# Six extra matmuls on TensorE ahead of the expert loop of a hybrid decoder step

## The reference

```python
expert = g_idx * EXPERTS_PER_GROUP + e_idx
combine = jnp.sum(jax.nn.one_hot(expert, N_EXPERTS, dtype=jnp.float32) * weight[..., None], axis=-2)
a = jnp.einsum('btd,edf->btef', h, w_gate)
u = jnp.einsum('btd,edf->btef', h, w_up)
z = jax.nn.silu(a) * u * combine[..., None].astype(a.dtype)
return jnp.einsum('btef,efd->btd', z, w_down).astype(h.dtype)
```

## Time and profile before

| | |
|---|---|
| median of the runs | 633.3 us (631.67 to 634.66) |
| profiled execution | 632.5 us |
| its span, first to last instruction | 630.8 us |
| mean granted TensorE clock | 0.893 |
| TensorE busy with matmuls | 474.5 us (75%) |
| VectorE, ScalarE, GpSimd busy | 222.8, 149.1, 109.6 us |
| DMA | 168.82 MB, mean 268 GB/s |

### The profile page before, as it was taken

One profiled execution on the slowest core, in us unless ns is written; L12 is line 12 of the kernel. 1 busy time (PEld: TensorE's weight loads), 2 busy tenths in 40 slices (PEclk: granted clock), 3 DMA queues, 4 the chain that ended last, 5 costly groups with the idle time before them and its releaser, 6 DMA issues.

```text
span 630.8 us, 8583 instructions
## 1 busy us (share of the span) xinstructions
PE 474.5 (75%) x2852; PEld 241.1 (38%) x2853; DVE 222.8 (35%) x544; ACT 149.1 (24%) x313; POOL 109.6 (17%) x171
## 2 busy tenths in 40 slices
PE   1869999999977999973006883758888889788290
PEld 0448777788533445432002331212333333233130
DVE  0341554142694288998500011001111111111188
ACT  1221444524755212230001111001111111111053
POOL 5030001000274450000610111011111111111000
PEclk9969999999999999986557897678999999899595
DMA  8994865410674923107961799999999999995432
GB/s 276 403 354 189 263 223 197 162 47 0 252 299 136 423 29 133 68 2 300 422 250 57 289 424 421 421 421 421 423 397 415 387 365 418 406 399 209 175 131 102
DMA packets 44414, 168.82 MB, mean 268 GB/s; under 512 B 11594, under 2 KB 20866, under 8 KB 29006
## 3 DMA queue, kind: packets, MB, share of 16 engines
q1 hardware_dynamic: 36682, 146.48, 59.2%
q0 software_dynamic: 7360, 21.88, 9.4%
q10 hardware_dynamic: 340, 0.09, 0.1%
HBM read 162.05 MB, written 15.71 MB: 282 GB/s over the span
## 4 chain that ended last, share of the span: by engine, by line
PE 55%; DMA 20%; DVE 11%; issue 7%; ACT 3%; SPq 2%; POOL 1%; POOLq 1%; DVEq 0%
PE B L1527 16%; PE B L1788 15%; DMA wB<-in_w_up 11%; PE B L1813 6%; PE B L1697 5%; DMA ada_m<-in_w_ada 4%; PE B L1464 2%; DMA ada<-in_w_ada 2%; PE B L1596 1%; PE B L1767 1%; PE B L1539 1%; PE B L1625 1%; PE B L1666 1%; POOL table L635 1%; PE B L1835 1%
## 5 line engine op out<-in xcount | busy, mean ns | idle before, releaser
L1788 PE MATMUL B<-wA,XT 128*32 128x512 f32 x480 | 117.8, 647 | 44.2 <-DMA wB<-in_w_up 24.9
L1788 PE MATMUL B<-wB,XT 128*32 128x512 f32 x480 | 117.8, 648 | 0.0
L1527 PE MATMUL B<-hT,win 128*128 128x256 f32 (+1 forms) x448 | 104.0, 392 | 2.0 <-DVE hT L999 2.0
L1527 PEld LDWEIGHTS B<-hT,win 128*128 128x128 f32 x448 | 86.1, 194 | 22.5 <-issue 9.4
L1788 PEld LDWEIGHTS B<-wA,XT 128*32 128x32 f32 x480 | 34.6, 118 | 124.1 <-issue 124.1
L1390 DVE TENSOR_TENSOR z<-silu_g,B 128x256 f32<-128x256 f32 x15 | 6.3, 421 | 157.6 <-ACT silu_g L886 157.6
L1813 PE MATMUL B<-wA,zT 128*32 128x512 f32 x240 | 54.9, 599 | 2.6 <-ACT zT L888 2.3
L1813 PE MATMUL B<-wB,zT 128*32 128x512 f32 x240 | 54.9, 600 | 0.0
L1767 PE MATMUL B<-ident,X 128*128 128x128 f32 x128 | 22.6, 305 | 35.2 <-DMA X<-h_dram,gidx 32.9
L1697 PE MATMUL B<-wout,yT 128*128 128x512 f32 x112 | 48.8, 593 | 0.0
L886 ACT ACTIVATE silu_g<-B 128x256 f32<-128x256 f32 x15 | 5.8, 384 | 150.8 <-PE B L1788 150.8
(11 more groups left out here) (377 smaller groups left out, 616.8 us busy)
## 6 DMA issues: line engine op xcount, KB each, us to landing
wB<-in_w_gate SPq DMA_DIRECT2D x24, 1024.0 KB, 12.8
wB<-in_w_up SPq DMA_DIRECT2D x24, 1024.0 KB, 17.7
wB<-in_w_down SPq DMA_DIRECT2D x24, 1024.0 KB
ada<-in_w_ada POOLq DMA_DIRECT2D x12, 1024.0 KB, 7.2
ada<-in_w_ada SPq DMA_DIRECT2D x8, 1024.0 KB, 11.8
wA<-in_w_gate SPq DMA_DIRECT2D x8, 1024.0 KB, 14.9
wA<-in_w_up SPq DMA_DIRECT2D x8, 1024.0 KB, 18.1
wA<-in_w_down SPq DMA_DIRECT2D x8, 1024.0 KB
```

Of the source, the lines that this page charges most:

```text
L1527: last = pe.matmul(B[(q % 2) * 2 + h][:, 0:cn], win[:, n % 3, k, col:col + P], hT[:, k, c0:c0 + cn], start=(k == 0), stop=(k == KD - 1))
L1788: last = pe.matmul(B[2][32 * g:32 * g + 32, :], XT[:, k, 32 * g:32 * g + 32], gu[:, :, k, :], start=(k == 0), stop=(k == KD - 1))
```

## The change

Between the last matmul of the ranks (L1762) and the function transpose_X, TensorE gets a wait and six matmuls. The wait is for idx_in, the semaphore that the read of the index table raises. The matmuls load the 128x128 identity and stream a [128, 512] block of wout, float32, for k = 0 to 5. Each writes the whole bank B[3] anew, nothing reads the result, and none raises a semaphore. All else is as before.

```diff
             last.then_inc(rank_ps, 1)
 
+            pe.wait_ge(idx_in, 16)
+            for k in range(6):
+                pe.matmul(B[3][:, :], ident[:, :], wout[:, k, 0:512], start=True, stop=True)
+
             def transpose_X(p, half):
```

## The result

The kernel with the six blocks took 629.4 us (median of eight runs, 628.12 to 630.51) against 633.5 us for the kernel before in the same runs (630.84 to 635.08): a ratio of 0.994, 95% interval 0.9919 to 0.9962. That is 4.1 us less.

A forecast was written before the change was run, and what follows sets the result against it. No single resource was taken to bound the kernel; until 339.2 the path was TensorE at half speed. Terms +1.7 - 0.9 - 0.74 = +0.06 us on 632.5 gave 632.6, or 633.4 against the median; range 630.2 to 635.5.

The forecast's parts named there:

- The chain and its bound: Whole kernel: no single resource bounds it; a shift in the first down projection's end counts in full.
- The added work: Ahead of the first transposes: six blocks are twelve matmuls taking 7.3 us, and transposes start 1.7 us late.
- the transposes' gain: First eight transposes, at the high clock: 0.90 us back, with bounds of 0 and 0.90.
- the blocks' delay: First transposes, held up by the blocks: 1.7 us late (1.25 to 2.4), counted on the path.
- The pause: Between transposes and first gate and up: stays 2.52 us, loses the clock; gate and up 8.80 us, 0.74 back.
- clock kept: Rival: clock outlasts the pause ahead of gate and up, which takes 7.11 us; 631.7, or 630.7 with shorter pause; chance 0.32.
- The rule on the pauses: TensorE's pauses: three of three over 2.3 us lost the clock, none under 2 us did.
- The transposes at the high clock: First eight transposes: 1.04 us at the high clock against 1.94, despite the skill's rule; 0.90 us back.
- The steps behind keep their pauses and their low stretches: Steps behind the first gate and up: pauses and low-clock stretches unchanged, no term in the sum.
- The slow side of the forecast: Slower than the range: clock never rises (638.0), or late rise plus a later pause's fall (1.69 us each); chance 0.11.

The follow-up runs named there:

- e3_hold: Kernel before, without the six blocks, plus two blocks in step 0 between gate and up and the next transposes: 632.5 us against 631.6, ratio 1.0000.
- e1_nine: Changed kernel with nine blocks in place of six ahead of the first transposes: 633.4 us, ratio 1.0003 to the kernel before.
- e2_keep: Changed kernel plus one block at the end of every step, behind the down projection: 629.5 us, ratio 0.9922 to the kernel before.

## Why the prediction was wrong, point by point

**The chain and its bound** were right. An earlier end of the first down projection reached the end in full: the stretch from there to step 5 differs by 0.1 us.

**The added work** was right in its size: twelve matmuls (7.24 to 8.09 us in five profiles, against 7.3 worked out), transposes some 2 us behind the landing of the rows. It was right, too, that a float32 block is two matmuls. (Ahead of the prediction the description of the loop gives 64 and 32 matmuls for a step; these are instructions of the trace, and the code has 32 and 16 calls.) What was wrong is its price. "They then end 1.7 - 0.9 = 0.8 us later than now" was added to the path. The start of gate and up isn't bound to the transposes' end but to the landing of the rows, some 4.5 us on, and the delay (1.6 to 2.5 us in five profiles, against 1.7) cost nothing. So the bound of nothing that stood for the transposes' gain was the true value, and by the same reason the true value for the blocks' delay. The sum had +1.7 - 0.9 = +0.8 us where the profiles have -0.16 (a to b).

**The pause** is the step that failed. The prediction kept its length at 2.52 us by a likeness with the pause of 2.62 us behind the first down projection, and reasoned that the blocks don't fill it. From this it took the clock as lost and gate and up at 8.80 us; it was 7.07 in all five profiles. With a fixed start and later transposes it had to shrink: 2.5 less what the blocks and transposes end later. It was 1.0 to 1.8 us in the five profiles of six. By the prediction's own rule, pauses under 2 us hold the clock, so with the right length the same rows would have given 7.11 us for gate and up and -2.4 us in all, 630.9 against the median. The measured 629.4 lies 1.5 us below even that, and this part stays open. The rival "clock kept" named the shortened pause, and had a quarter of 0.32.

**The rule on the pauses** was half right: three of three over 2.3 us lost the clock in the profile before. The count left out the pause of 2.18 us ahead of 437.93, which the chain books as a wait for wB, and behind which gate and up took 8.80 us as well. In the changed one 2.98 us (ahead of 353.80, 7.11 us) held, in e3_hold 3.03 us held, in e1_nine 3.01 us lost it, and in e2_keep 1.95 us. The length alone doesn't decide, and no run shows what does. "Lost in the pause" is also loosely said: behind the pause of 2.62 us in the profile before, the granted clock was 1.00 until 356.4 and 0.50 from there, 1.1 us into gate and up.

**The transposes at the high clock** went as the row said: 0.90 us in the changed kernel, with a granted clock of 1.00. The Trainium skill, page "TensorE: Matmul & The Clock Gate", section "PE-mode transpose", says that full clock doesn't engage for transposes; the trace disagrees for these float32 ones. Whether transposes by themselves raise the clock no run shows. It was still worth nothing, as the start behind them is fixed.

**The remaining 1.5 us** of the 4.1 were in no term. "The steps behind keep their pauses and their low stretches" doesn't hold of the profiles: their low stretches move from one execution to the next, in the kernel before too. The slow side of the forecast allowed for such a move, against the kernel; in the profiles it was for it in sum (-0.75, -1.22, +0.84). That the six are the cause isn't shown.

## What to carry to other kernels

An idle TensorE ahead of a burst on the path can be given work to bring its clock up, but what counts is the pause right ahead of the burst: the filler has to reach into it. Before a delay is priced, find what the next start is bound to; compare two profiles in which the work ahead differs, and see whether the start moves. A float32 matmul of 512 columns counted double here, so count the trace's instructions and not the code's calls.

## What the runs showed that was not expected

- From the issue of the gather to the first gate and up it took 8.7 to 9.1 us in all kernels but the one with nine blocks, though the transposes took 0.9 to 1.96 us and the blocks ahead of them ended up to 2.6 us behind the landing of the rows.
- A pause of 3.4 us (three blocks) brought the clock from 1.00 to 0.50 inside itself; one of 3.03 us (e3_hold) held it, one of 1.95 us (e2_keep) lost it.
- The scatter of the runs is not only the clock's falls behind the change: from the issue of the first gather to the end the four profiles before lie within 1.7 us of each other and the five with six within 2.3, while in the latter that issue itself came anywhere from 324.03 to 327.87.
